# Activation blocks of seven experts turned by transfers and VectorE in place of TensorE

## The chip, the cores and the metric

One core of one Trainium2 chip runs the whole program. The metric is the device time of one execution in microseconds (us), as a median over several runs.

## The reference

Two layers on 256 rows of width 1024, all in float32. Layer 0 has sliding-window and forgetting attention and a dense SwiGLU; layer 1 has differential attention and then a mixture of eight experts, of which each row uses two. Each sublayer ends in a layer norm. The change touches only the experts:

```python
def swiglu(x, w_gate, w_up, w_down):
    return jnp.dot(jax.nn.silu(jnp.dot(x, w_gate)) * jnp.dot(x, w_up), w_down)
...
    def expert_block(args):
        xb, e = args
        return swiglu(xb, w_gate[e], w_up[e], w_down[e])
```

With D = 1024 and 3584 hidden columns an expert has three weight matrices of 14.7 MB each.

## The kernel before

**Units.** Weights stream from HBM in units of 128 x 2048 float32, 1 MB each. The sync engine (SP) loads them into 14 slots of `raw`, one after the other in one queue, each as soon as VectorE has finished with what was in the slot (line 416). ScalarE rounds a unit to float32r (`whi`, helper `hi`, line 1107), VectorE subtracts to get the remainder (`wlo`, helper `lo`, line 1434), and TensorE multiplies with three products per tile (`three`, lines 564 to 566). `whi` and `wlo` have three places, so unit j+3 can be rounded only when TensorE has finished unit j.

**An expert.** `EXP_ORDER` lists its 42 units: for each of seven blocks `c` of 512 hidden columns two units "gate" and two "up", and two "down" units that multiply the finished block. Before, the down units of block c-1 follow the gate and up units of block c. Experts 0 to 6 run in a loop on each engine (`expert(e)`), expert 7 is written out (`last`); a second pass (`again`) exists for the case that an expert gets over 128 rows and isn't executed here.

**A block.** Its 128 rows (partitions) x 512 columns lie in two PSUM banks. After the second up unit ScalarE writes silu of the gate sum to `htmp` and VectorE multiplies by the up sum (`gated`; semaphores `m_silu`, `m_h`; lines 1351 and 1834). TensorE then turns the block, four 128 x 128 tiles, into PSUM bank 4 (`hidden_t`, line 1013; semaphore `m_tr`), after the second gate unit of the next block. ScalarE rounds it into `hth` (`hidden_hi`, line 1355, `m_hi`), VectorE takes the remainder into `htl` (`hidden_lo`, line 1839, `m_lo`), and the down units wait for `m_lo`.

**Order.** Every engine's program is written out: at place j of the list ScalarE and VectorE handle unit j+3 and then whatever else stands at j. GpSimd (POOL), a queue of its own, fetches the next expert's rows from DRAM (`xg` from `x_slots`, four transfers, line 535), and VectorE turns them in 32 x 32 squares (`rows_turned`, line 1808) at places `ROWS_TURN`. Rows get into `x_slots` by four indirect transfers (line 527), and POOL waits for their landing (`x_put`) before the first fetch. SP also writes each expert's output rows (`y_rows`, line 445).

Of the kernel before, what the change touches and what calls it, by code (L numbers as in the profile page):

```python
# [30 lines left out]
P = 128  # L31
D = 1024
TOK = 256
# [91 lines left out]
TAIL_BANKS = (7, 4, 0, 2)  # L125
ROWS_TURN = (PER_EXP - 10, PER_EXP - 9)
PICK_AT = (26, 29, 32, 35)
# [3 lines left out]
def trunk(nc, x_in, w_dense, w_moe, cst, bias_cst, vec_rows, sinks, b_forget, lam_rows, subln, w_router, out):  # L131
    with ExitStack() as ctx:
# [3 lines left out]
        def sem(name):  # L136
            return ctx.enter_context(nc.semaphore(name))
# [85 lines left out]
        def expert_hidden(c, f):  # L223
            if c < EC - 1:
                return hth[:, f * P:(f + 1) * P], htl[:, f * P:(f + 1) * P]
            return xth[:, f, P:TOK], xtl[:, f, P:TOK]

        def expert_hidden_all(c):
            if c < EC - 1:
                return [t[:, :].rearrange("p (k n) -> p k n", k=4) for t in (hth, htl)]  # L230
            return [t[:, 0:4, P:TOK] for t in (xth, xtl)]

# [94 lines left out]
        m_hi = sem("expert_hidden_hi")  # L327
        m_lo = sem("expert_hidden_lo")
        xr_out = sem("x_rows_written")
        y_out = sem("expert_out_rows_written")  # L330
# [83 lines left out]
        def _(sp):  # L414
# [67 lines left out]
        def _(pool):  # L482
# [77 lines left out]
        def _(pe):  # L560
# [446 lines left out]
            def expert(e, last=False, again=False):  # L1007
# [14 lines left out]
                for j, (what, c, half) in enumerate(EXP_ORDER):  # L1022
# [76 lines left out]
        def _(act):  # L1099
# [248 lines left out]

            def gated(e, j, c):
                act.wait_ge(w_used, e * PER_EXP + (N_DENSE + j + 1))  # L1350
                A(htmp[:, :], ps[c % 2][:, :], ACT.Silu).then_inc(m_silu, 1)

            def hidden_hi(e, c):
                act.wait_ge(m_tr, e * EC + (c + 1))
                A(expert_hidden_all(c)[0], ps[4][:, :].rearrange("p (k n) -> p k n", k=4), ACT.Copy).then_inc(m_hi, 1)

            def expert(e, last=False, again=False):
                for j, (what, c, half) in enumerate(EXP_ORDER):
                    s, n = moe_slot(j + SPLIT_AHEAD)
                    if (what, half, c) == ("up", 1, EC - 1):  # L1360
                        gated(e, j, c)
                    if j == PER_EXP - 4:
                        hidden_hi(e, EC - 1)
# [17 lines left out]
                    if (what, half) == ("up", 1) and c < EC - 1:  # L1381
                        gated(e, j, c)
                    if (what, half) == ("gate", 1) and c:
                        hidden_hi(e, c - 1)
                    if j == PER_EXP - 3 and not last:
                        gathered(e + 1)
# [35 lines left out]
        def _(dve):  # L1422
# [408 lines left out]

            def gated(e, c):
                dve.wait_ge(m_silu, e * EC + (c + 1))
                dve.tensor_tensor(htmp[:, :], htmp[:, :], ps[2 + c % 2][:, :], ALU.mult).then_inc(m_h, 1)

            def hidden_lo(e, c):
                dve.wait_ge(m_hi, e * EC + (c + 1))
                h, l = expert_hidden_all(c)
                dve.tensor_tensor(l, ps[4][:, :].rearrange("p (k n) -> p k n", k=4), h.bitcast(F32),
                                  ALU.subtract).then_inc(m_lo, 1)  # L1840
# [8 lines left out]
            def expert(e, last=False, again=False):  # L1849
                for j, (what, c, half) in enumerate(EXP_ORDER):  # L1850
# [8 lines left out]
                    if (what, half, c) == ("up", 1, EC - 1):  # L1859
                        gated(e, c)  # L1860
                    if j == PER_EXP - 4:
                        hidden_lo(e, EC - 1)
# [4 lines left out]
                    if (what, half) == ("up", 1) and c < EC - 1:  # L1867
                        gated(e, c)
                    if j in ROWS_TURN and not (last or again):
# [9 lines left out]
                    if (what, half) == ("gate", 1) and c:  # L1879
                        hidden_lo(e, c - 1)  # L1880
# [202 lines left out]
```

## Time and profile before

| | |
|---|---|
| median of 3 runs | 1396.49 us (1396.47 to 1397.69) |
| the profiled execution's own time | 1397.27 us |
| span from its first to its last instruction | 1395.5 us |
| mean granted TensorE clock | 0.997 |
| TensorE busy | 1375.8 us, 99% |
| VectorE busy | 1128.7 us, 81% |
| ScalarE busy | 958.4 us, 69% |
| GpSimd busy | 53.3 us, 4% |
| DMA | 444.77 MB, mean 319 GB/s |

The experts run from about 434 us to the end. The profile is one execution. Its engines are PE (matmul), PEld (weight load of TensorE), DVE (VectorE), ACT (ScalarE), POOL (GpSimd) and SP (sync); a q behind the name is the engine's instruction queue, where issues of transfers stand. Of the span, 99% is PE busy, but the ends of matmuls are modelled, so a stretch is better measured from the start of one matmul to the start of another.

### The profile page before, as it was taken

Reading aid. Unit: us, or ns where it says so; the run is one execution under the profiler, and the core shown is the slowest. Engines: PE = TensorE matmul, PEld = TensorE weight load, DVE = VectorE, ACT = ScalarE, POOL = GpSimd, SP = SyncE. Lnnn points to the kernel's source line nnn. Section 1 sums busy time; section 2 is a strip of 40 time slices with the busy share of each in tenths; the row PEclk is TensorE's granted clock in tenths of the full one; section 3 lists DMA queues with packets and bytes.
Section 4 is the critical chain, followed back from the end, with each engine's and each line's share of the span. In section 5 each row is a group of like instructions: output and inputs, shape, how many; then the busy total and the mean of one; then the engine's idle time right before and its main releaser. Section 6 shows DMA issues by size and latency. Waiting matters only on the chain.

```text
span 1395.5 us, 18790 instructions
## 1 busy us (share of the span) xinstructions
PE 1375.8 (99%) x6942; PEld 1156.8 (83%) x6942; DVE 1128.7 (81%) x1007; ACT 958.4 (69%) x892; POOL 53.3 (4%) x74
## 2 busy tenths in 40 slices
PE   9999999999999999999999999999999999999996
PEld 9988888889888888888888888888888888888874
DVE  5647555565668889889988998988998898899997
ACT  6655544455657777777877777777777777778774
POOL 1200000000003000000000000000000000000200
PEclk9999999999999999999999999999999999999998
DMA  9834655535157999999999999999999999999950
GB/s 369 355 120 182 212 181 181 185 147 192 51 212 317 394 421 396 423 421 400 416 417 377 369 391 375 371 417 381 369 380 391 373 372 414 375 368 370 393 239 32
DMA packets 65266, 444.77 MB, mean 319 GB/s; under 512 B 7800, under 2 KB 8080, under 8 KB 13760
## 3 DMA queue, kind: packets, MB, share of 16 engines
q1 hardware_dynamic: 60192, 425.96, 77.9%
q0 software_dynamic: 4880, 18.08, 3.7%
q8 instruction: 32, 0.52, 0.1%
q14 instruction: 18, 0.15, 0.0%
q10 hardware_dynamic: 144, 0.07, 0.0%
HBM read 431.48 MB, written 12.59 MB: 318 GB/s over the span
## 4 chain that ended last, share of the span: by engine, by line
PE 92%; DVE 5%; ACT 2%; issue 0%; DMA 0%; SPq 0%; DVEq 0%; ACTq 0%
PE ps L564 26%; PE ps L566 26%; PE ps L565 26%; PE ps L623 6%; PE ps L624 3%; PE ps L1013 2%; DVE wlo L1434 1%; ACT raw L1163 1%; ACT whi L1107 1%; PE ps L776 1%; PE ps L718 1%; DVE raw L1469 1%; PE ps L593 1%; ACT biasb L1142 0%; DVE x L1601 0%
## 5 line engine op out<-in xcount | busy, mean ns | idle before, releaser
L1434 DVE TENSOR_TENSOR wlo<-raw,whi 128x2048 fp32r<-128x2048 f32 x396 | 904.7, 2290 | 169.6 <-ACT whi L1107 168.9
L1107 ACT ACTIVATE whi<-raw 128x2048 fp32r<-128x2048 f32 x397 | 760.3, 1918 | 234.2 <-PE ps L566 227.9
L564 PE MATMUL ps<-whi,xt 128*128 128x512 f32 (+1 forms) x1096 | 432.4, 395 | 2.8 <-DVE wlo L1434 1.7
L566 PE MATMUL ps<-whi,xt 128*128 128x512 f32 (+1 forms) x1096 | 425.8, 388 | 0.0
L565 PE MATMUL ps<-wlo,xt 128*128 128x512 f32 (+1 forms) x1096 | 425.2, 388 | 0.0
L564 PEld LDWEIGHTS ps<-whi,xt 128*128 128x128 f32 x1096 | 205.9, 188 | 48.8 <-DVE wlo L1434 6.7
L566 PEld LDWEIGHTS ps<-whi,xt 128*128 128x128 f32 x1096 | 205.8, 188 | 43.4
L565 PEld LDWEIGHTS ps<-wlo,xt 128*128 128x128 f32 x1096 | 206.1, 188 | 40.2
L564 PE MATMUL ps<-whi,hth 128*128 128x512 f32 x464 | 181.6, 391 | 0.5 <-DVE wlo L1434 0.5
L566 PE MATMUL ps<-whi,htl 128*128 128x512 f32 x464 | 180.8, 390 | 0.0
L565 PE MATMUL ps<-wlo,hth 128*128 128x512 f32 x464 | 180.6, 389 | 0.0
L623 PE MATMUL ps<-xt,whi 128*128 128x512 f32 x352 | 124.7, 399 | 0.3 <-issue 0.3
L564 PEld LDWEIGHTS ps<-whi,hth 128*128 128x128 f32 x464 | 87.1, 188 | 18.7 <-DVE wlo L1434 0.7
L566 PEld LDWEIGHTS ps<-whi,htl 128*128 128x128 f32 x464 | 87.1, 188 | 18.5
L565 PEld LDWEIGHTS ps<-wlo,hth 128*128 128x128 f32 x464 | 87.2, 188 | 17.6
L624 PE MATMUL ps<-xt,wlo 128*128 128x256 f32 x352 | 98.8, 281 | 0.0
L623 PEld LDWEIGHTS ps<-xt,whi 128*128 128x128 f32 x352 | 66.1, 188 | 16.8 <-ACT xt L1122 0.5
L624 PEld LDWEIGHTS ps<-xt,wlo 128*128 128x128 f32 x352 | 66.5, 189 | 0.3
L564 PE MATMUL ps<-xt,whi 128*128 128x256 f32 x232 | 66.4, 286 | 0.3 <-issue 0.3
L565 PE MATMUL ps<-xt,whi 128*128 128x256 f32 x232 | 65.6, 283 | 0.0
L566 PE MATMUL ps<-xt,wlo 128*128 128x256 f32 x232 | 65.6, 283 | 0.0
L564 PEld LDWEIGHTS ps<-xt,whi 128*128 128x128 f32 x232 | 44.4, 192 | 1.7 <-issue 0.9
(258 smaller groups left out, 847.3 us busy)
## 6 DMA issues: line engine op xcount, KB each, us to landing
raw<-w_moe SPq DMA_DIRECT2D x336, 1024.0 KB, 7.7
raw<-w_dense SPq DMA_DIRECT2D x61, 1024.0 KB, 4.8
x_slots<-hth POOLq DMA_DIRECT2D x16, 256.0 KB, 13.1
raw<-vec_rows POOLq DMA_DIRECT2D x4, 1024.0 KB, 6.8
y_rows<-work SPq DMA_DIRECT2D x8, 512.0 KB, 8.5
biasb<-x_slots POOLq DMA_DIRECT2D x28, 128.0 KB, 6.9
raw<-w_dense SPq DMA_DIRECT2D x4, 512.0 KB, 6.9
x<-x_in SPq DMA_DIRECT2D x2, 512.0 KB, 5.3
```

The source lines that it names most:

```text
L564: mm(o, lh, rh, start=start, stop=False)
L565: mm(o, lh, rl, start=False, stop=False)
L566: return mm(o, ll, rh, start=False, stop=stop)
L593: r = pe.transpose(ps[bank][:, i * P:(i + 1) * P], src[:, tb, kt * P:(kt + 1) * P], ident)
L623: mm(ps[bank + b][:, :], h[:, kt, c], xt[:, kt, :, :], start=kt == 0, stop=False)
L624: r = mm(ps[bank + b][:, 0:TOK], l[:, kt, c], xth[:, kt, :], start=False, stop=kt == KT - 1)
L718: r = mm(bank[:, c0:c0 + nk], q, kk, start=True, stop=True)
L776: r = mm(o, PT[g][:, kt, h * P:(h + 1) * P], v, start=kt == 0, stop=kt == qblk)
L1013: r = pe.transpose(ps[4][:, i * P:(i + 1) * P], htmp[:, i * P:(i + 1) * P], ident)
L1107: A(unit(whi, j), raw[:, slot * UNIT:(slot + 1) * UNIT], ACT.Copy).then_inc(hi_rdy, 1)
L1163: A(PROB[g][:, h, 0:nk], PROB[g][:, h, 0:nk], ACT.Exp, bias=negm[:, g % 2, h:h + 1], accum_out=sm[:, g % 4, h:h + 1]).then_inc(e_rdy, 1)
L1434: dve.tensor_tensor(unit(wlo, j), raw[:, slot * UNIT:(slot + 1) * UNIT], unit(whi, j).bitcast(F32), ALU.subtract).then_inc(lo_rdy, 1)
```

## The change

In experts 0 to 6, blocks 0 to 5 are no longer turned by TensorE. `gated` writes them in another column order to `h_rows` (two buffers), sixteen transfers of 32 partitions x 128 columns (16 KB each) move them to `h_moved`, eight issued by SP (semaphores `h_in`) and eight by POOL (`h_in2`), VectorE turns 32 x 32 squares into `h_turned` (`hidden_squares`), and `hidden_hi` and `hidden_lo` read that in place of PSUM. Block 6 and expert 7 are turned by TensorE as before. The down units of a block come one block later, so the weight stream is in another order too. In the new list the last up unit of blocks 0 to 6 stands at 3, 7, 11, 17, 23, 29 and 35, and the down units of blocks 0 to 6 begin at 12, 18, 24, 30, 36, 38 and 40. VectorE turns at 8, 12, 16, 22, 28 and 34; ScalarE rounds one place later; VectorE takes the remainder at 9, 13, 18, 24, 30 and 36. `ROWS_TURN` moves to 31 and 32, and TensorE turns block 6 after unit 37 in place of 38.

```diff
-    if _c:
-        EXP_ORDER += [("down", _c - 1, 0), ("down", _c - 1, 1)]
-EXP_ORDER += [("down", EC - 1, 0), ("down", EC - 1, 1)]
+    if _c > 1:
+        EXP_ORDER += [("down", _c - 2, 0), ("down", _c - 2, 1)]
+for _c in (EC - 2, EC - 1):
+    EXP_ORDER += [("down", _c, 0), ("down", _c, 1)]
+
+MOVED = EC - 1
+UP_END = [EXP_ORDER.index(("up", _c, 1)) for _c in range(EC)]
+MOVE_AT = {UP_END[_c] + 4: _c for _c in range(MOVED)}
+SQUARES_AT = {UP_END[_c] + 5: _c for _c in range(MOVED)}
+HIDDEN_AT = {UP_END[_c] + 6: _c for _c in range(MOVED)}
+REST_AT = {UP_END[_c] + (6 if _c < 2 else 7): _c for _c in range(MOVED)}
...
-ROWS_TURN = (PER_EXP - 10, PER_EXP - 9)
+ROWS_TURN = (PER_EXP - 11, PER_EXP - 10)
...
+        h_rows = [htmp[:, :], spare[:, 512:1024]]
+        h_moved = [spare[:, 1024:1536], spare[:, 1536:2048]]
+
+        def hidden_move(engine, c, groups, done):
+            for q in groups:
+                for u in range(4):
+                    engine.dma_start(h_moved[c % 2][32 * q:32 * q + 32, P * u:P * u + P],
+                                     h_rows[c % 2][32 * u:32 * u + 32, P * q:P * q + P]).then_inc(done[c % 2], 16)
+
+        h_turned = [acc[:, 0, 0:512], acc[:, 0, 512:1024]]
...
+                    if j in MOVE_AT:
+                        sp.wait_ge(m_h, e * EC + (MOVE_AT[j] + 1))
+                        hidden_move(sp, MOVE_AT[j], (0, 1), h_in)
                     sp.wait_ge(lo_rdy, e * PER_EXP + (N_DENSE + j + 1))
                     load(w_moe[e * PER_EXP + (SLOTS + j)], moe_slot(SLOTS + j)[0])
...
+                for c in range(MOVED):
+                    pool.wait_ge(m_h, (n - 1) * EC + c + 1)
+                    hidden_move(pool, c, (2, 3), h_in2)
...
-                    if (what, half) == ("gate", 1) and c:
+                    if (what, half) == ("gate", 1) and c and (last or again):
                         hidden_t(c - 1)
-                    if j == PER_EXP - 4:
+                    if j == PER_EXP - 5:
                         hidden_t(EC - 1)
...
+            def hidden_squares(e, c):
+
+                dve.wait_ge(h_in[c % 2], e * (128 * MOVED // 2) + 128 * (c // 2 + 1))
+                dve.wait_ge(h_in2[c % 2], e * (128 * MOVED // 2) + 128 * (c // 2 + 1))
+                if c == 0:
+                    dve.wait_ge(x_put, 16 * 2 * TB)
+                if c > 1:
+                    dve.wait_ge(m_lo, e * EC + (c - 1))
+                dve.transpose(h_turned[c % 2].rearrange("p (f u s) -> p f u s", f=4, u=4),
+                              h_moved[c % 2].rearrange("p (u f r) -> p f u r", f=4, u=4)).then_inc(m_tr, 1)
...
                     if j < PER_EXP - 3 or not last:
                         lo(e * PER_EXP + (N_DENSE + j + SPLIT_AHEAD + 1), j, moe_slot(j + SPLIT_AHEAD)[0])
                     if (what, half) == ("up", 1) and c < EC - 1:
-                        gated(e, c)
+                        gated(e, c, not (last or again))
+                    if j in SQUARES_AT and not (last or again):
+                        hidden_squares(e, SQUARES_AT[j])
+                    if j in REST_AT and not (last or again):
+                        hidden_lo(e, REST_AT[j], True)
```

On ScalarE `gated` and `hidden_hi` change in the same way, `hidden_hi` standing behind the rounding of unit j+3 at the places `HIDDEN_AT`.

## Rows read from the trace of the kernel before

**Rows 1.** The page: busy us (share of the span) x instructions of each engine.
```profile
PE 1375.8 (99%) x6942; PEld 1156.8 (83%) x6942; DVE 1128.7 (81%) x1007; ACT 958.4 (69%) x892; POOL 53.3 (4%) x74
```

**Rows 2.** The page: the chain that ended last, shares of the span by line.
```profile
PE ps L564 26%; PE ps L566 26%; PE ps L565 26%; PE ps L623 6%; PE ps L624 3%; PE ps L1013 2%; DVE wlo L1434 1%; ACT raw L1163 1%; ACT whi L1107 1%; PE ps L776 1%; PE ps L718 1%; DVE raw L1469 1%; PE ps L593 1%; ACT biasb L1142 0%; DVE x L1601 0%
```

**Rows 3.** Waits, whole span: waiter and releaser: us in total, times, longest.
```profile
DVE wlo L1434 <- ACT whi L1107: 168.9, 268, 5.8
...
PEld ps L564 <- DVE wlo L1434: 7.5, 14, 1.1
```

**Rows 4.** Timeline of PE in expert 0: start, us, engine, line, operation.
```profile
451.23 0.39 PE L566 MATMUL ps<-whi,xt 128*128 128x512 f32 x1
451.46 0.60 PE L1013 MATMUL ps<-con,htmp 128*128 128x128 f32 x4
451.81 0.47 PE L564 MATMUL ps<-whi,xt 128*128 128x512 f32 x1
```

**Rows 5.** Timeline of ACT in expert 0, units 8, 9, 11 and 14.
```profile
451.65 1.92 ACT L1107 ACTIVATE whi<-raw 128x2048 fp32r<-128x2048 f32 x1 [0.80 <-PE ps L566]
...
454.84 1.92 ACT L1107 ACTIVATE whi<-raw 128x2048 fp32r<-128x2048 f32 x1 [0.78 <-PE ps L566]
...
460.28 1.92 ACT L1107 ACTIVATE whi<-raw 128x2048 fp32r<-128x2048 f32 x1 [0.32 <-PE ps L566]
...
468.44 1.92 ACT L1107 ACTIVATE whi<-raw 128x2048 fp32r<-128x2048 f32 x1 [0.80 <-PE ps L566]
```

**Rows 6.** Timeline of DVE in expert 0: block 0, and units 7 and 11.
```profile
450.38 0.68 DVE L1834 TENSOR_TENSOR htmp<-htmp,ps 128x512 f32<-128x512 f32 x1
450.97 2.28 DVE L1434 TENSOR_TENSOR wlo<-raw,whi 128x2048 fp32r<-128x2048 f32 x1
...
462.31 2.29 DVE L1434 TENSOR_TENSOR wlo<-raw,whi 128x2048 fp32r<-128x2048 f32 x1
```

**Rows 7.** Groups by line, whole span: busy us, mean ns of one.
```profile
L1013 PE MATMUL ps<-con,htmp 128*128 128x128 f32 x224 | 33.5, 271 | 0.0
...
L1808 DVE STREAM_TRANSPOSE ps<-biasb 128x512 f32<-128x512 f32 x14 | 9.9, 708 | 0.0
```

**Rows 8.** Weight loads by SP, line 416: issued in 448 to 454, then 960 to 980.
```profile
DMA to landing us min/median/max: 27.8/28.1/28.4
...
DMA to landing us min/median/max: 4.7/4.8/4.9
```

**Rows 9.** Output rows by SP, line 445: all seven, then the one of 440 to 450.
```profile
L445 SPq DMA_DIRECT2D y_rows<-work x7: 356/356/371, 443.9 to 1150.6; - x7
...
DMA to landing us min/median/max: 23.4/23.4/23.4
```

**Rows 10.** POOL: timeline in expert 0; line 535 landings at 460 to 470, 640 to 1140.
```profile
448.63 2.67 POOL L527 DMA_INDIRECT x_slots<-acc,x_to  x1 [0.30 <-issue]
464.45 2.29 POOL L535 DMA_DIRECT2D biasb<-x_slots  x4 [13.15 <-DMA x_slots<-acc,x_to]
...
DMA to landing us min/median/max: 6.4/8.0/9.8
...
DMA to landing us min/median/max: 4.8/6.6/11.0
```

**Rows 11.** Stretch 600 to 640 (last: DMA share, GB/s); POOL's queue, 760 to 780.
```profile
600.00:640.00 40.00, 40.00 (x184) 33.09 (x183) 35.26 (x19) 29.36 (x20) 0.00 (x0) 1.00 1.01 423
...
q0 software_dynamic: 192, 0.52, 9.5%
```

**Rows 12.** Stretches at the end (columns as before, third from last PEclk); first matmuls (line 571).
```profile
1385.00:1388.00 3.00, 0.00 (x0) 0.00 (x0) 3.00 (x8) 2.11 (x4) 0.00 (x0) 0.80 0.02 5
1388.00:1390.00 2.00, 0.00 (x0) 0.00 (x0) 1.93 (x5) 0.85 (x3) 0.00 (x0) 0.50 0.04 8
...
L571 PE MATMUL ps<-con x80: 272/275/275, 6.0 to 425.5; 128*128 128x128 f32 x80
...
L571 PE MATMUL ps<-htmp x18: 274/421/581, 1.1 to 4.7; 128*128 128x128 f32 x18
```

More of the change, by code:

```diff
@@ L223, in expert_hidden @@
         def expert_hidden(c, f):
-            if c < EC - 1:
+            if c < EC - 1 and c % 2 == 0:
                 return hth[:, f * P:(f + 1) * P], htl[:, f * P:(f + 1) * P]
-            return xth[:, f, P:TOK], xtl[:, f, P:TOK]
+            f0 = 4 if c < EC - 1 else 0
+            return xth[:, f0 + f, P:TOK], xtl[:, f0 + f, P:TOK]
         def expert_hidden_all(c):
-            if c < EC - 1:
+            if c < EC - 1 and c % 2 == 0:
                 return [t[:, :].rearrange("p (k n) -> p k n", k=4) for t in (hth, htl)]
-            return [t[:, 0:4, P:TOK] for t in (xth, xtl)]
+            f0 = 4 if c < EC - 1 else 0
+            return [t[:, f0:f0 + 4, P:TOK] for t in (xth, xtl)]
+        h_rows = [htmp[:, :], spare[:, 512:1024]]
[6 more added lines that the diff above has]
+        h_turned = [acc[:, 0, 0:512], acc[:, 0, 512:1024]]
         def part_bank(q):
@@ L328, in trunk @@
         m_lo = sem("expert_hidden_lo")
+        h_in = [sem(f"expert_hidden_first_half_moved_{i}") for i in range(2)]
+        h_in2 = [sem(f"expert_hidden_second_half_moved_{i}") for i in range(2)]
         xr_out = sem("x_rows_written")
@@ L1347, in gathered, with gated, hidden_hi @@
                 r.then_inc(ga_hi, 1)
-            def gated(e, j, c):
+            def gated(e, j, c, moved):
                 act.wait_ge(w_used, e * PER_EXP + (N_DENSE + j + 1))
-                A(htmp[:, :], ps[c % 2][:, :], ACT.Silu).then_inc(m_silu, 1)
-            def hidden_hi(e, c):
+                if moved:
+                    A(h_rows[c % 2].rearrange("p (q f r) -> p f q r", q=4, f=4),
+                      ps[c % 2][:, :].rearrange("p (f q r) -> p f q r", q=4, f=4), ACT.Silu).then_inc(m_silu, 1)
+                else:
+                    A(htmp[:, :], ps[c % 2][:, :], ACT.Silu).then_inc(m_silu, 1)
+            def hidden_hi(e, c, moved=False):
                 act.wait_ge(m_tr, e * EC + (c + 1))
-                A(expert_hidden_all(c)[0], ps[4][:, :].rearrange("p (k n) -> p k n", k=4), ACT.Copy).then_inc(m_hi, 1)
+                A(expert_hidden_all(c)[0], (h_turned[c % 2] if moved else ps[4][:, :]).rearrange("p (k n) -> p k n", k=4),
+                  ACT.Copy).then_inc(m_hi, 1)
             def expert(e, last=False, again=False):
@@ L1360, in expert @@
                     if (what, half, c) == ("up", 1, EC - 1):
-                        gated(e, j, c)
-                    if j == PER_EXP - 4:
+                        gated(e, j, c, False)
+                    if j == PER_EXP - 5:
                         hidden_hi(e, EC - 1)
@@ L1381, in expert @@
                     if (what, half) == ("up", 1) and c < EC - 1:
-                        gated(e, j, c)
-                    if (what, half) == ("gate", 1) and c:
+                        gated(e, j, c, not (last or again))
+                    if (what, half) == ("gate", 1) and c and (last or again):
                         hidden_hi(e, c - 1)
+                    if j in HIDDEN_AT and not (last or again):
+                        hidden_hi(e, HIDDEN_AT[j], True)
                     if j == PER_EXP - 3 and not last:
@@ L1859, in expert @@
                     if (what, half, c) == ("up", 1, EC - 1):
-                        gated(e, c)
-                    if j == PER_EXP - 4:
+                        gated(e, c, False)
+                    if j == PER_EXP - 5:
                         hidden_lo(e, EC - 1)
@@ L1867, in expert @@
                     if (what, half) == ("up", 1) and c < EC - 1:
-                        gated(e, c)
+                        gated(e, c, not (last or again))
[3 more added lines that the diff above has]
+                        hidden_lo(e, REST_AT[j], True)
                     if j in ROWS_TURN and not (last or again):
@@ L1878, in expert @@
                         dve.tensor_copy(slot_tok[:, :], ps[7][:, 256:257]).then_inc(ix_rdy, 1)
-                    if (what, half) == ("gate", 1) and c:
+                    if (what, half) == ("gate", 1) and c and (last or again):
                         hidden_lo(e, c - 1)
```

13 lines of the change are left out of this document (9 added, 4 removed).

## The prediction

> **What bounds the kernel now.** I read the page first: TensorE is busy for 99% of the span and VectorE for 81% [rows 1], and the chain that ended last runs nearly all over the matmul lines, with 2% on the turning line L1013 [rows 2]. The waits say the same: TensorE waited for VectorE's remainders 14 times, 7.5 us in all, while VectorE waited 168.9 us for ScalarE, which itself waits for TensorE to give a place back [rows 3]. So a microsecond off TensorE's stream is a microsecond off the time, as long as the three engines' loop and the transfers keep up. What a change costs is therefore read where the new waits end: in VectorE's queue (which makes `wlo`) and at `m_lo`.
>
> **Slack of the loop.** Call T(j) the moment at which ScalarE takes unit j+3, just after TensorE ended unit j. A unit lasts 2.72 us: units 11 and 14 are taken at 460.28 and 468.44 [rows 5], a third of 8.16. Rounding takes 1.92 [rows 5], the remainder 2.29 [rows 6], with 0.03 between: it is there at T(j)+4.24. TensorE begins the next unit some 0.19 before the T of the last (its next matmul could start 0.23 after 451.23, ScalarE starts at 451.65 [rows 4, 5]), so it needs unit j+3 at T(j)-0.19+5.44 = T(j)+5.25. VectorE may be 1.0 us late, not more.
>
> **Part 1, the turning removed: -19.7 us.** Without turning T advances by 2.72; over one turning it advances 454.84-451.65 = 3.19 [rows 5]. One block costs 0.47 us. (PE's own starts give 0.58-0.23 = 0.35 and a slower next matmul [rows 4], together 0.44.) Six blocks in seven experts are 42, 42 x 0.47 = 19.7; by the lower figure 18.5. The 224 matmuls of line 1013 at 271 ns [rows 7] would make far more, 42 x 4 x 0.271 = 45.5, but they overlap; the starts decide. The Trainium skill, page "VectorE: DVE Perf Modes", section "Rules for kernel authors", advises TensorE for a 128 x 128 transpose when PSUM will do, which speaks against this change, and its section on the three paths gives TensorE 390 ns (bf16): by that figure the four-tile turnings would cost 168 x 0.39 = 65.5 us, where the trace has 19.7.
>
> **Part 2, VectorE's new work: hidden, 0.** Each block adds one turn of squares, 0.708 [rows 7], of which 0.09 overlaps the neighbour as `gated` does (450.38+0.68 against 450.97 [rows 6]): 0.62. A unit with one extra step takes VectorE 2.20+0.60, 2.8 to 2.85, 0.1 more than TensorE's 2.72. The longest run of such units is places 28 to 32 (squares, `gated`, remainder, two `rows_turned`): 5 x 0.12 = 0.6, under the 1.0 of slack. If the regrouped reads and writes run 20% slower (no row shows them), it costs some tenths an expert. I take 0 here, at most +3 in all. ScalarE's work is the same in amount and is hidden as before. SP issues 8 transfers a block at 0.36 [rows 9], 2.9 us in 16 us in which it only waits; the loads behind them go out 3 us later, with 11 units in hand.
>
> **Part 3, block 5 comes too late for unit 38: +14.2 us.** The down units of block 5 are 38 and 39, directly behind those of block 4, but VectorE takes its remainder at place 36, behind the remainder of unit 39. That one can't be there before T(36)+4.24; ScalarE has silu of block 6 and the rounding of block 5 in the same two units (two of 0.6 beside two of 1.92 in 5.44), which makes it some 0.1 later. Then 0.68 less overlap: `m_lo` comes at T(36)+5.0. TensorE would begin unit 38 at T(36)-0.19+2.72 = T(36)+2.53. The gap is 2.5 us; the turning of block 6 (0.47, after unit 37) falls into it. Net 2.03, times seven experts 14.2. Before, place 38 took the last block's remainder ahead of the unit's own; now that holds for block 6 only. The other blocks have a place or more to spare: block 0 is due at unit 12 and is taken at 9, at T(9)+4.9, where TensorE comes at T(9)+5.25.
>
> **Part 4, the first move stands behind the weight queue: +15.3 us.** At the start of the experts the loads are far behind: those issued at 448 to 454 land 28.1 us later, while in 960 to 980 it is 4.8 [rows 8]. Is that the queue, or only the loads? The write of output rows, of another kind but issued by SP at 443.9, also took 23.4 us [rows 9]: whatever SP issues waits its turn. POOL's transfers of that time land after 6.4 to 9.8 [rows 10], so its queue is not behind that backlog. Now block 0 of expert 0: `m_h` comes at 450.38+0.68 = 451.1 [rows 6]. SP's eight moves go out until 454 and stand behind a load issued at 450.5, which lands at 478.5; the moves at about 479.5. POOL's half comes no earlier: POOL first waits for the rows' landing until 464.45, issues four fetches in 2.29 [rows 10], then eight moves at 0.55 until 471.2; with 6.4 to 9.8 to land, 477.6 to 481. VectorE stands at the squares from the end of unit 11's remainder, 462.31+2.29 = 464.6 [rows 6], less the turning that is gone: 464.1. Queued behind it on VectorE are units 12 and up, which TensorE wants. TensorE ends unit 11 at 468.44-0.47-0.19 = 467.8 [rows 5]. After 479.5 come the squares (0.62), unit 12's remainder (2.20), block 0's remainder (0.68), and unit 12 is a down unit that needs both: 483.1. TensorE is idle for 15.3 us; with the two landings as bounds, 13.5 to 17. In the kernel before nothing in TensorE's path waits for this queue within 30 us, so nothing is paid back later.
>
> **Part 5, the clock after it: +1.8 us.** At the end the granted clock goes from 1.00 to 0.80 and 0.50 (2.4 to 1.2 GHz) once TensorE has stopped [rows 12]. The first 18 matmuls of the kernel, from 1.1 to 4.7 us, lasted 421 ns in the median and up to 581, where the same line later takes 275 [rows 12]: about 3.6 us at half pace, 1.8 lost. I take the same here once; between 0 and 4.
>
> **Part 6, the blocks after: +2 us.** While TensorE stands, the queue shortens, but SP keeps loading up to 12 units ahead, so the moves of blocks 1 to 5 still stand behind 4 to 5 MB. `m_h` comes at T(j)+4.8 and VectorE reaches the squares at T(j+5)+4.24: 13.0 us for issue and landing. After the stop the loads in front of each block's moves land 11 to 12.5 us after `m_h`: a margin under 1.5, plus the 1.0 of slack. Does the queue drain? TensorE needs 117.8 an expert (443.9 to 1150.6 over six [rows 9]), less 6 x 0.47, plus 2.03: 117.0. The transfers: 42 MiB at 423 GB/s, the rate while the queue is full [rows 11], 104.1; output rows 1.2; the fetched rows 1.9 (0.52 MB in 9.5% of 20 us [rows 11]). The moves, 0.26 MB a block, cost 0.62 at that rate, 0.95 at the price of the fetch (32 partitions too, but pieces twice as large, nearest in kind), 1.9 if half the piece doubles that. With 0.95 the sum is 112.9: it drains 4 us an expert, and small waits of experts 0 and 1 make about 2 us; bounds 0 and 6.
>
> **The sum.** -19.7 + 0 + 14.2 + 15.3 + 1.8 + 2.0 = +13.6 against the profiled execution's 1397.3 (span 1395.5 and 1.8 around it): 1410.9. The median lies 0.8 below that execution: 1410.1.
>
> **Rivals.**
> (a) The transfers bind, slower still. At 1.9 us a block the sum of part 6 is 118.6 an expert against 117.0, and the moves' landing holds VectorE in every expert: +1.6 x 7 = 11, 1421. POOL's half can do it alone: eight issues are 4.4 us, and a landing of 11.0, the longest [rows 10], makes 15.4 against 13.0, so 2.4 less 1.0 = 1.4 late; in a third of the 42 blocks that is 20, 1430. For it: 672 small transfers. Against: a landing of 6.6 in the median gives 11.0 us, in time; it decides at 14 us.
> The Trainium skill, page "DMA: Bandwidth & Descriptors", section "Bandwidth", calls transfers under 64 KB descriptor-dominated and gives 0.68 us for 4 KB and 0.95 for 64 KB: an estimate of sixteen at 0.7 one after another would be 11.2 us a block, 67 an expert, 57 over what TensorE's pace leaves, and about 1810 us. No run here shows transfers of 16 KB in a row; if they overlap the rule doesn't bite, and a bit of (a)'s chance is for it.
> (b) Faster: the moves of block 0 are not held by the queue (they land within 13 us, as POOL's fetches did). Then parts 4 to 6 vanish: 1410.1-19.1 = 1391.0. Against: the 23.4 us of the output rows, and POOL's start at 466.7, which alone gives a wait. It decides whether landing is before 465.
> (c) No wait at unit 38, if VectorE runs further ahead than I read: 1410.1-14.2 = 1395.9, no change. Against: unit 39 can't be rounded before unit 36 has ended, whatever VectorE does.
> (d) Neither, the change as it is meant: 1397.3-19.7-0.8 = 1376.8.
>
> **How the numbers follow.** My case 0.60, with 1400 to 1420 for itself (part 4 +-2, part 3 +-3, part 6 and clock +-4); (a) 0.20; (b) 0.08; (c) 0.07; (d) 0.05. Faster by over 0.2% (2.8 us, about what a measurement here can tell): (b) and (d), 0.13. Within it: (c) and a sliver of mine, 0.09. Slower: 0.78. The range leaves out (b) and (d) below and the far part of (a) above: 1394 to 1428.
>
> **What would show it.** L1013 with 56 matmuls in place of 224; 42 squares more on VectorE. Part 4: one idle time of TensorE of 14 to 17 us near 468, VectorE's squares waiting for a transfer, a granted clock of 0.5 in that stretch. Part 3: seven idle times of about 2.5 us on TensorE, one an expert, ended by VectorE's remainder of a block. Parts 2 and 6: no waits for transfers from expert 2 on; many of them would speak for (a). I am wrong if SP's small moves overtake its loads, or if VectorE's regrouped steps take much over 0.7 us.

## The result and the profile after the change

| | before | after |
|---|---|---|
| median of 4 runs | 1397.09 us (1396.47 to 1397.99) | 1472.94 us (1472.10 to 1473.60) |
| span of the profiled execution | 1395.5 us | 1470.7 us |
| mean granted TensorE clock | 0.997 | 0.980 |

The ratio is 1.0542 (95% interval 1.0529 to 1.0555): 75.8 us slower. The forecast was 13.6 us slower, with a range up to 1428, so the side was right and the size far off. First the page of the kernel after: busy us (share) x instructions, the chain that ended last by engine and by line, and the weight loads with their median us to landing.

```profile
PE 1385.9 (94%) x6774; PEld 1144.3 (78%) x6774; DVE 1145.9 (78%) x1049; ACT 956.3 (65%) x892; POOL 218.3 (15%) x410
...
PE 49%; DMA 22%; DVE 12%; SPq 9%; issue 4%; ACT 3%; DVEq 0%; ACTq 0%
PE ps L593 13%; PE ps L595 12%; PE ps L594 12%; DMA biasb<-htmp 12%; DMA biasb<-biasb 9%; SPq L249 8%; DVE wlo L1470 7%; PE ps L652 6%; PE ps L653 3%; ACT whi L1136 2%; DMA raw<-w_dense 1%; ACT raw L1192 1%; PE ps L805 1%; PE ps L747 1%; DVE htmp L1872 1%
...
raw<-w_moe SPq DMA_DIRECT2D x336, 1024.0 KB, 12.7
```

TensorE was busy for 99% [rows 1] and made nearly the whole chain [rows 2]; now it makes half. The moves (`biasb<-htmp` and `biasb<-biasb` are the two buffers) and SP's issuing of them (L249) are 29% of it. The waits of the kernel after, as in [rows 3] (us in total, times, longest):

```profile
DVE acc L1885 <- DMA biasb<-htmp: 49.0, 15, 19.5
...
DVE acc L1885 <- DMA biasb<-biasb: 25.0, 19, 2.2
```

That is 74.0 us in 34 of 42 blocks, where I had foreseen one wait and a few small ones. The lines L1470, L1872, L1885 and L1891 here are the remainder, `gated`, `hidden_squares` and `hidden_lo`. VectorE (DVE) in the third expert, the stretches of its squares, shows what nearly every block looks like:

```profile
746.06 0.68 DVE L1872 TENSOR_TENSOR htmp<-htmp,ps 128x512 f32<-128x512 f32 x1
...
762.71 0.71 DVE L1885 STREAM_TRANSPOSE acc<-biasb 128x512 f32<-128x512 f32 x1 [2.83 <-DMA biasb<-htmp]
...
780.30 0.71 DVE L1885 STREAM_TRANSPOSE acc<-biasb 128x512 f32<-128x512 f32 x1 [1.73 <-DMA biasb<-biasb]
...
798.21 0.71 DVE L1885 STREAM_TRANSPOSE acc<-biasb 128x512 f32<-128x512 f32 x1 [2.06 <-DMA biasb<-htmp]
```

**Where the 75 us of span lie.** The issues of `y_rows` stand one expert apart. Before, they come at 443.9 and then every 117.8 us; after, at 444.9, 591.3, 717.3, 843.5, 969.7, 1094.0 and 1220.1. Expert 0 takes 146.4, the next five 125.8 each. From the last of them to the end it is 250.6, before 244.9. So: 1.0 up to the experts, 28.6 in expert 0, 5 x 8.0 = 40.0 in the next five, 5.7 in the last two: 75.3.

### The profile page after: what moved, and what is told of

Read it like the earlier page. It is cut to its first block, busy times and chain, and to the rows that moved or that the text cites. A ratio compares the mean times of both kernels' runs of the same rounds, so it can differ in the third digit from the quotient of the medians.

```text
span 1470.7 us, 19231 instructions
## 1 busy us (share of the span) xinstructions
PE 1385.9 (94%) x6774; PEld 1144.3 (78%) x6774; DVE 1145.9 (78%) x1049; ACT 956.3 (65%) x892; POOL 218.3 (15%) x410
## 4 chain that ended last, share of the span: by engine, by line
PE 49%; DMA 22%; DVE 12%; SPq 9%; issue 4%; ACT 3%; DVEq 0%; ACTq 0%
PE ps L593 13%; PE ps L595 12%; PE ps L594 12%; DMA biasb<-htmp 12%; DMA biasb<-biasb 9%; SPq L249 8%; DVE wlo L1470 7%; PE ps L652 6%; PE ps L653 3%; ACT whi L1136 2%; DMA raw<-w_dense 1%; ACT raw L1192 1%; PE ps L805 1%; PE ps L747 1%; DVE htmp L1872 1%
## 5 line engine op out<-in xcount | busy, mean ns | idle before, releaser
L1470 DVE TENSOR_TENSOR wlo<-raw,whi 128x2048 fp32r<-128x2048 f32 x396 | 899.3, 2284 | 153.2 <-ACT whi L1136 151.6
L593 PE MATMUL ps<-whi,xt 128*128 128x512 f32 (+1 forms) x1288 | 515.9, 401 | 48.3 <-DVE xt L1891 24.8
L594 PE MATMUL ps<-wlo,xt 128*128 128x512 f32 (+1 forms) x1288 | 505.4, 392 | 0.0
L595 PE MATMUL ps<-whi,xt 128*128 128x512 f32 (+1 forms) x1288 | 505.3, 392 | 0.0
L593 PEld LDWEIGHTS ps<-whi,xt 128*128 128x128 f32 x1288 | 244.9, 190 | 124.6 <-DVE wlo L1470 48.6
L595 PEld LDWEIGHTS ps<-whi,xt 128*128 128x128 f32 x1288 | 244.9, 190 | 52.9
L594 PEld LDWEIGHTS ps<-wlo,xt 128*128 128x128 f32 x1288 | 245.4, 191 | 47.2
L249 POOL DMA_DIRECT2D biasb<-htmp x168 | 82.4, 499 | 381.1 <-DVE htmp L1872 380.4
L593 PE MATMUL ps<-whi,hth 128*128 128x512 f32 x272 | 108.0, 397 | 19.8 <-DVE htl L1891 19.4
L249 POOL DMA_DIRECT2D biasb<-biasb x168 | 82.2, 497 | 254.0 <-DVE biasb L1872 246.4
L595 PE MATMUL ps<-whi,htl 128*128 128x512 f32 x272 | 106.8, 393 | 0.0
L594 PE MATMUL ps<-wlo,hth 128*128 128x512 f32 x272 | 106.7, 392 | 0.0
L1885 DVE STREAM_TRANSPOSE acc<-biasb 128x512 f32<-128x512 f32 x42 | 29.9, 711 | 74.1 <-DMA biasb<-htmp 49.0
L652 PEld LDWEIGHTS ps<-xt,whi 128*128 128x128 f32 x352 | 66.1, 188 | 16.8 <-ACT xt L1151 0.5
## 6 DMA issues: line engine op xcount, KB each, us to landing
raw<-w_moe SPq DMA_DIRECT2D x336, 1024.0 KB, 12.7
```

The costliest lines, as they stand in the source:

```text
L249: engine.dma_start(h_moved[c % 2][32 * q:32 * q + 32, P * u:P * u + P], h_rows[c % 2][32 * u:32 * u + 32, P * q:P * q + P]).then_inc(done[ ...
L593: mm(o, lh, rh, start=start, stop=False)
L594: mm(o, lh, rl, start=False, stop=False)
L595: return mm(o, ll, rh, start=False, stop=stop)
L652: mm(ps[bank + b][:, :], h[:, kt, c], xt[:, kt, :, :], start=kt == 0, stop=False)
L1470: dve.tensor_tensor(unit(wlo, j), raw[:, slot * UNIT:(slot + 1) * UNIT], unit(whi, j).bitcast(F32), ALU.subtract).then_inc(lo_rdy, 1)
```

## The experiments

Two explanations stood against each other for the many waits. "Full": the transfers of an expert take longer in sum than TensorE does, whatever is waited for (the forecast's rival (a), far above its price). "Late": each move only takes too long to land, since it is issued late and stands behind loads. They differ when a move is made but not waited for, and when it gets more time. Times are medians; each ratio is to the kernel before, run beside it (1397.1 to 1397.6 us). Runs e1, e2b, e6 to e9, e11 and e14 move or load something else than the kernel needs, so what they compute is not the reference's.

### The moves taken away: e1 and e6

Without the moves, VectorE turns squares of what `gated` wrote; e6 also takes block 5's remainder ahead of unit 39's.

```diff
-                if j in MOVE_AT: ... hidden_move(sp, MOVE_AT[j], (0, 1), h_in)
-            for c in range(MOVED): ... hidden_move(pool, c, (2, 3), h_in2)
-                dve.wait_ge(h_in[c % 2], ...); dve.wait_ge(h_in2[c % 2], ...)
+                dve.wait_ge(m_h, e * EC + (c + 1))
# e6 also
+                    if REST_AT.get(j) == MOVED - 1 and not (last or again):
+                        hidden_lo(e, MOVED - 1, True)
                     if j < PER_EXP - 3 or not last:
                         lo(...)
```

> The changed kernel without its sixteen transfers a block: VectorE turns the squares straight out of the block as it was written (the output is then not the reference's), at the same places, and nobody waits for a transfer. It gives what the transfers cost in all and what is left. Both theories (late: the transfers' landing comes after VectorE's place; full: the transfers take the 16 DMA engines' time) say the same here: the 19.7 us of TensorE's turnings gone, the wait at unit 38 left at 2.5 us an expert, so 1391 us; if that idle time drops TensorE's clock in every expert as the trace after shows (0.5 for 3.4 us), up to 12 more, 1403.

> e1_no_moves with the remainder of block 5 taken at place 36 ahead of the remainder of unit 39 in place of behind it (the output isn't the reference's, as there). My part 3: the wait at unit 38 (2.2 us here, and half a clock behind it in four experts) goes, so 1398.8 - 7 x 2.0 - 4 x 1.4 = 1379, and the 19.7 us of the turnings show for the first time. Rival: VectorE's fuller queue is what ate the gain; then the time stays within 3 us of 1398.8.

e1: 1398.76 us, ratio 1.0014 (1.0003 to 1.0025). e6: 1376.99, ratio 0.9849 (0.9833 to 0.9866). So all but 1.7 of the 75.8 us come with the moves. e6 is 20.2 under before: that is the turning's worth, 19.7 in the forecast, with VectorE's new work at nothing. The difference of the two, 21.8 us, is block 5 coming late to unit 38. The wait is in the trace of e1 as forecast, 2.2 us in each of seven experts, and behind it stands a cost that I had not put down. Waits of the weight loads (PEld), then two stretches of expert 0 (third number from last: the granted clock):

```profile
PEld ps L587 <- DVE xt L1884: 15.2, 7, 2.2
```

```profile
541.00:545.00 4.00, 3.60 (x11) 2.85 (x12) 3.22 (x3) 0.90 (x1) 0.00 (x0) 0.74 1.00 386
545.00:549.00 4.00, 4.00 (x16) 3.22 (x15) 1.38 (x1) 2.08 (x2) 0.00 (x0) 0.83 1.01 422
```

In four of the seven experts the clock falls to 0.50 (1.2 GHz) for some 3.3 us just after this short stop. TensorE works through that time at half pace: 4 x 3.3 / 2 = 6.6, and 15.2 + 6.6 = 21.8.

### The moves made, but their data not needed: e2b, e7, e8, e9, e11

Here the transfers read a constant and write to buffers that nobody reads; the squares are those of e1. Each is still checked for its landing, but later: before the squares of blocks 3 and 4 VectorE waits for the moves of blocks 0 to 3, and at the end of an expert for the rest. e2b makes all sixteen a block, e7 SP's eight alone, e8 POOL's eight alone. e9 makes four of 128 partitions x 128 columns (64 KB), two by each; e11 two of 32 partitions x 512 columns (64 KB) by SP.

```diff
-    engine.dma_start(h_moved[c % 2][32 * q:32 * q + 32, P * u:P * u + P],
-                     h_rows[c % 2][32 * u:32 * u + 32, P * q:P * q + P])
+    engine.dma_start(h_dump[c % 4][32 * q:32 * q + 32, P * u:P * u + P],
+                     con[32 * u:32 * u + 32, P * q:P * q + P])
# e9, one for each q
+    engine.dma_start(h_dump[c % 4][:, P * q:P * q + P], con[:, P * q:P * q + P])
# e11, one for each q, SP alone
+    engine.dma_start(h_dump[c % 4][32 * q:32 * q + 32, :], con[32 * q:32 * q + 32, 0:512])
# all five, in hidden_squares (shown for e2b)
+                if c in (3, 4):
+                    dve.wait_ge(h_in[c - 3], e * (128 * MOVED // 2) + 256)
+                    dve.wait_ge(h_in2[c - 3], e * (128 * MOVED // 2) + 256)
```

> As e1_no_moves, but the sixteen transfers a block are issued by SP and POOL at their places, with a constant table as their source and dumps that nobody reads; VectorE only makes sure far later that they have landed (the output isn't the reference's). Late: only the waiting hurt, so the time is that of e1_no_moves within 5 us. Full: the transfers fill the DMA engines, the weight loads fall behind, ScalarE comes to wait for weights, and the time stays near 1450.

> e2b_unawaited with SP's eight transfers a block alone, POOL's left out (output not the reference's). Its price a block is read from how fast the queue of weight loads drains: landing of loads (28 us at the start), where 10.3 us an expert go in the kernel before. If price goes with bytes (0.62 us a block for all sixteen), nothing is seen: 1399. If the two halves share the 3.2 us a block that the full queue implies, 1.6 each, the sum is 107 + 10 = 117 an expert, just TensorE's pace: 1399 to 1405 with the landing staying near 25. If SP's half is the dear one (the trace after shows the rate falling to 300 GB/s for five microseconds when it passes), 2.5 us: 122 an expert, about 1425.

> e2b_unawaited with POOL's eight transfers a block alone, SP's left out (output not the reference's). Even shares: as e7. If SP's half is the dear one, POOL's costs 0.7 us a block, the queue drains by 6 us an expert, and the time is that of e1_no_moves, 1399.

> e2b_unawaited with the same 0.26 MB a block in the same 512-byte rows, but as four transfers of 128 partitions x 128 columns, two by SP and two by POOL, in place of sixteen of 32 partitions (output not the reference's). If the price is per byte or per row, it stays that of e2b_unawaited, 1458. If it is per transfer or by the 32 partitions that each touches, it falls to a quarter, 0.8 us a block: 1399 to 1402, and the queue drains.

> e7_sp_half_unawaited with SP's eight transfers of 32 partitions x 128 columns a block replaced by two of 32 partitions x 512 columns: the same 0.13 MB, the same 32 partitions each, a quarter of the count (output not the reference's). If each transfer from SP has its price, the 2.25 us a block fall to 0.6 and the time is that of e1_no_moves, 1399. If the price lies in touching 32 partitions at a time, it stays at 1425.

| | us | ratio (interval) | us per expert |
|---|---|---|---|
| e2b, all sixteen | 1457.72 | 1.0433 (1.0402 to 1.0463) | 127.5 |
| e7, SP's eight | 1425.44 | 1.0199 (1.0178 to 1.0219) | 122.9 |
| e8, POOL's eight | 1398.37 | 1.0008 (0.9998 to 1.0018) | 118.2 |
| e9, four of 64 KB | 1398.97 | 1.0012 (1.0001 to 1.0022) | 118.0 |
| e11, two tall ones by SP | 1400.98 | 1.0029 (1.0018 to 1.0039) | 118.3 |

e2b is still 59 us slower than e1, where "late" had it near e1. But the time alone doesn't settle the question, since the late check was not late enough. VectorE's waits for moves in e2b, then in e7, and ScalarE's for weights in e2b:

```profile
DVE acc L1888 <- DMA acc<-con: 43.7, 11, 6.7
```

```profile
DVE acc L1884 <- DMA acc<-con: 26.1, 11, 5.7
```

```profile
ACT whi L1137 <- DMA raw<-w_moe: 24.2, 20, 2.3
```

In every expert of both runs the squares of block 3 stood for moves of the block before (and at times those of block 4), and those waits are as large as most of what the two runs lose against e1 (59 and 27 us). e8, e9 and e11 have none. What speaks for "full" is the queue. If the moves were only late, the backlog of loads would drain as it does in e1, and faster, since the experts last longer; in e2b it never does, and ScalarE comes to wait for weights 20 times, which neither e1 nor the kernel before shows in the experts. Landing of SP's loads in e2b at 960 to 980 us, where the kernel before had 4.8 in the median [rows 8]:

```profile
DMA to landing us min/median/max: 20.6/27.7/29.5
```

The kernel after says the same of itself. Landing of all its loads issued from 560 to 1290 us:

```profile
DMA to landing us min/median/max: 6.3/12.8/16.6
```

Where the queue has run empty a load lands after 4.7 [rows 8]; here none does in six experts, so it is never empty. e14, below, closes the question.

**The price of a move.** A load's landing time is the backlog in front of it. While that is well above 4.7 us, it shrinks in each expert by TensorE's period less the time that the transfers need. Loads of e1 issued at 460 to 480 us, then at 700 to 720:

```profile
DMA to landing us min/median/max: 25.2/25.9/26.9
...
DMA to landing us min/median/max: 7.6/8.4/9.2
```

17.5 us in 240 us, which are 2.03 periods of 118.2: 8.6 an expert, so without moves the transfers need 109.6. (I had 107.2 from the rate of the full queue.) The same for e8, at 460 to 480 and 1060 to 1080:

```profile
DMA to landing us min/median/max: 29.0/29.2/29.5
...
DMA to landing us min/median/max: 9.1/9.5/10.4
```

19.7 in 5.08 periods is 3.9: they need 114.3, and six blocks make 4.7, 0.8 a block for POOL's eight. e9 gives 25.4 at 520 to 540 and 11.0 at 1060 to 1080, 3.1 an expert, 0.9 a block. e11 gives 28.0 and 22.7, 1.0 an expert, 1.3 a block. In e7 and e2b the backlog doesn't shrink, so the period is what the transfers need, whoever waits: (122.9 - 109.6) / 6 = 2.2 a block for SP's eight, (127.5 - 109.6) / 6 = 3.0 for all; and 2.2 + 0.8 = 3.0. By the same rule the kernel after gives a little less, (125.8 - 109.6) / 6 = 2.7; its moves read and write other buffers than those of e2b, and whether that makes the difference isn't shown. The prices are good to about 0.1 us a block, since the landing time also moves by 1 or 2 us within an expert. A transfer of 16 KB by SP thus takes 0.28 us from all the others, one by POOL 0.10, where its bytes at 423 GB/s [rows 11] are 0.04. Of SP's tall ones (32 partitions, 64 KB) each takes 0.65, so the median of e11, which lies between its two expectations, tells little, and the drain tells that neither the count alone nor the bytes alone set the price.

The packets show one difference between the two queues. Queues on the pages of e8, then of e7: packets, MB, share of 16 engines (q1 is SP's, q0 POOL's; without moves they have 60192 and 4880):

```profile
q1 hardware_dynamic: 60192, 425.96, 77.7%
q0 software_dynamic: 15632, 23.60, 5.1%
```

```profile
q1 hardware_dynamic: 76320, 431.48, 80.0%
q0 software_dynamic: 4880, 18.08, 3.5%
```

336 moves are 16128 packets by SP, 48 each, and 10752 by POOL, 32 each. A price of 2.8 times is more than the packets' 1.5 times; what the rest is stays open.

### More time for the moves, or a shorter queue: e3, e4, e5, e14

e3 takes squares, rounding and remainder of blocks 1 to 4 two places later. e4 turns expert 0 by TensorE. e5 is e6's reordering with the moves left in. e14 loads three quarters of the unit in 294 of the 336 loads of expert weights (all but the first 14 and the last 28).

```diff
# e3
+LATER = (0, 2, 2, 2, 2, 0)
+SQUARES_AT = {UP_END[_c] + 5 + LATER[_c]: _c for _c in range(MOVED)}   # HIDDEN_AT, REST_AT alike
# e4, on each engine
+            for e in range(1):
+                expert(e, plain=True)
+            with dve.Fori(1, N_EXP - 1) as e:
# e14
+                sp.dma_start(raw[:, s * UNIT:s * UNIT + 3 * UNIT // 4], src[:, 0:3 * UNIT // 4]).then_inc(loaded[s], 16)
```

> The changed kernel with squares, rounding and remainder of blocks 1 to 4 two places (5.4 us) later, where their down units leave room. Late: the waits of 1.7 to 2 us before the squares of these blocks go, some 6 us an expert, 42 in all, 1432. Full: the landing moves out with the place, since the loads in front go out sooner; no change, 1465 to 1473.

> The changed kernel with expert 0 written out and its blocks turned by TensorE; experts 1 to 6 as in the change. Expert 0 took about 146 us where it took 118. Late: 28 us less, 1445, if the queue has drained below VectorE's 13 us by expert 1. Full: the queue still holds 17 us of loads at expert 1, the first block there waits some 5 to 7 us, 1452.

> The changed kernel with the remainder of block 5 ahead of unit 39's, the edit that gave 21.8 us where no transfers ran. Full: TensorE's wait at unit 38 was time in which the weight queue caught up, so most of the gain is given back at the squares of the next blocks: 1465 to 1473, a gain under 8. Late (each wait stands for itself): 1473 - 21.8 = 1451.

> The changed kernel, transfers and waits untouched, with every weight load of experts 0 to 6 cut to three quarters of its unit (the rest of the slot keeps old data; the output isn't the reference's). Full: an expert's transfers fall from 126 to about 100 us, under TensorE's 117, the queue empties, the waits at the squares go from expert 1 on, and the time comes down to that without moves plus the first block's wait, 1399 + 17 + 2 = 1418, less where the smaller loads have shortened the first queue too. Late (issue of 5 us and a landing that comes with any transfer, against 13.0): 1455 or more.

**e3**: 1495.14 us, ratio 1.0701 (1.0644 to 1.0757), 22 us above the kernel after. The waits of blocks 1 to 4 went, as "late" had it, but block 5 paid for them all: five microseconds more for four of six blocks brought nothing. That it got worse neither explanation had foreseen. VectorE's waits:

```profile
DVE acc L1886 <- DMA biasb<-biasb: 63.0, 7, 10.4
DVE acc L1886 <- DMA biasb<-htmp: 18.8, 1, 18.8
```

The time that was owed in four or five pieces, some 8 us an expert, is paid in one piece of 9 at block 5, whose squares were not moved. The sum is about the same, 81.8 against 74.0. But TensorE now stands for longer at a time, and the clock stays at half longer behind it: the end of the stop in the third expert and 8 us behind it:

```profile
820.00:824.00 4.00, 0.00 (x0) 0.00 (x0) 0.00 (x0) 0.00 (x0) 0.00 (x0) 0.74 1.01 291
824.00:828.00 4.00, 1.12 (x4) 0.72 (x4) 3.33 (x3) 2.58 (x3) 0.00 (x0) 0.50 1.01 420
828.00:832.00 4.00, 0.99 (x2) 0.83 (x3) 4.00 (x5) 2.13 (x2) 0.00 (x0) 0.50 1.00 418
```

Its mean granted clock is 0.960, against 0.980. During the long stop SP has nothing to load, and the queue even runs empty for a while (in every expert some loads land in 4.7 or 4.8 us), so the 129.0 us an expert of e3 aren't set by the sum of the transfers alone.

**e4**: 1456.78, ratio 1.0426 (1.0370 to 1.0482). That is nearer to the 1452 of "full" than to the 1445 of "late", and slower than both. The first wait isn't gone but comes one expert later, at 11.3 us in place of 19.5, in an expert of 137.0; the next four take 125.5 each, like those of the kernel after. **e5**: 1470.81, ratio 1.0526 (1.0505 to 1.0547). The edit that was worth 21.8 us without the moves is worth 2.1 with them: TensorE gets to the next block sooner and waits there. The squares of block 0, which the kernel after has in time from expert 1 on, now wait 3.1 to 3.4 us in each of these experts. That is how a bound by the transfers looks.

**e14**: 1415.33, ratio 1.0131 (1.0110 to 1.0151). Of all waits of the squares one is left, in expert 0:

```profile
DVE acc L1888 <- DMA biasb<-htmp: 14.0, 1, 14.0
```

With the sixteen moves as they are and a quarter less to load, experts 1 to 5 take 118.2 each, as in e1. It is therefore their sum with the loads that makes the waits of all later blocks, not the moves' own landing.

### POOL alone: e12, e10, e13, and the order alone: e15

```diff
# e12
-                        hidden_move(sp, MOVE_AT[j], (0, 1), h_in)
-                    hidden_move(pool, c, (2, 3), h_in2)
+                    hidden_move(pool, c, range(4), h_in2)
# e10 also (blocks 0, 5 and 6 by TensorE)
-MOVED = EC - 1
+MOVED = (1, 2, 3, 4)
+SQUARES_AT = {UP_END[_c] + 7: _c for _c in MOVED}
# e13 also (expert 0 by TensorE)
-                for c in MOVED:
+                for c in (MOVED if n > 1 else ()):
# e15
+MOVED = ()
```

> The changed kernel with all sixteen transfers of a block issued by POOL. If SP's eight are what fills the queue, the price a block falls from 3.0 to about 1.6 us and what is left is: 1398.8 without moves, one long wait at the first block of expert 0 (POOL is free at 467.8, issues until 476, landing by 484: some 18 us and 2 of clock), and issue and landing of 8 + 5.7 us against 13.0, a wait of up to 1 us a block less slack: 1420 to 1440. If the number of transfers is what counts, whoever issues them: 1465 or more.

> A version meant to beat both: only blocks 1 to 4 are moved (TensorE turns 0, 5 and 6), POOL issues all sixteen transfers of a block and SP none, and the squares stand two places later (18.4 us after the block is written, where POOL needs 8 to issue and 6 to 8 to land). 28 turnings less at 0.47 are 13.2 us; no wait at unit 38; the first block of expert 0 is some 3 us late at the squares: 1387. If sixteen of POOL's transfers are as dear as SP's eight (over 2.2 us a block), the queue of loads stays full: 1400 or more.

> e10_four_by_pool with expert 0 written out and turned by TensorE throughout. There one stall of TensorE in expert 0, ended by POOL's first moves, and the half clock behind it cost some 9 to 10 us; expert 0 gives up four turnings, 1.9 us. So 1391.2 - 9.5 + 1.9 = 1383.6. If the queue of loads, which stayed at 21 us there, is the bound that ate the difference (sixteen small transfers by POOL fill what TensorE's pace leaves), the time stays at 1390 or more.

> The new order of the weight stream and of the down units alone: no block is moved, TensorE turns all seven in every expert. The order costs nothing: 1397 within 2. If it costs (down units of blocks 5 and 6 back to back), up to 7 us more.

**e12**: 1494.74 us, ratio 1.0697 (1.0676 to 1.0719). The first expectation missed. The second had "1465 or more" if the number of transfers fills the queue; the time fits, but the cause is another. If POOL's price is 1.6 a block for sixteen, the transfers need 109.6 + 9.6 = 119.2, and indeed the loads land after 7.2 us in the median: this kernel isn't full. It is late. POOL and VectorE in the third expert:

```profile
728.51 0.68 DVE L1868 TENSOR_TENSOR htmp<-htmp,ps 128x512 f32<-128x512 f32 x1
...
745.47 0.71 DVE L1880 STREAM_TRANSPOSE acc<-biasb 128x512 f32<-128x512 f32 x1 [3.20 <-DMA biasb<-htmp]
```

```profile
729.48 7.84 POOL L249 DMA_DIRECT2D biasb<-htmp x16 [39.70 <-DVE htmp L1868]
```

`m_h` comes at 729.2. Sixteen issues take 7.84 us, up to 8.6 go by until landing, and the squares begin at 745.5, 16.3 us after `m_h`, where 13.0 are to be had. So there are two bounds, and each half of the moves meets one: from SP they are too dear, from POOL they take too long to issue.

**e10** goes between them: four blocks, squares two places later, all by POOL. 1391.20, ratio 0.9956 (0.9940 to 0.9973), 4 us above what was expected. One wait is left, 6.4 us in expert 0, as e13 takes it away: **1384.18 us, ratio 0.9906 (0.9890 to 0.9923)**, no wait of the squares at all, 13 us faster than before and 89 faster than the kernel after. In e13 the loads' landing neither falls nor grows, 21.8 us in the median at 960 to 980, so its period of 116.0 from expert 1 on is again what the transfers need: (116.0 - 109.6) / 4 = 1.6 a block for POOL's sixteen, twice the 0.8 of e8. **e15**, the new order with all blocks turned by TensorE: 1396.58, ratio 0.9996 (0.9986 to 1.0005). The order costs nothing by itself.

## Why the prediction was right or wrong

| step | forecast | measured | from |
|---|---|---|---|
| part 1, turning gone | -19.7 | -20.2 | e6 against before |
| part 2, VectorE's new work | 0 | in the -20.2 | e6 |
| part 3, unit 38 | +14.2 | +21.8 | e1 against e6 |
| parts 4 and 5, first wait, clock | +17.1 | about +21 | see below |
| part 6, blocks after | +2.0 | about +53 | the rest |
| sum | +13.6 | +75.8 | |

The last line but one is a remainder, and the terms don't add as the table has them: once the transfers bind, TensorE's wait at unit 38 is time that they use too. e5 takes that wait away from the kernel after and gains 2.1 us of the 21.8.

**Part 1** held: what counts is the start of the next matmul, not the 271 ns of each turning. By the 390 ns of the Trainium skill's page "VectorE: DVE Perf Modes", section "The three transpose paths", the forecast's estimate was 65.5 us; e6 gives a third of it. The advice of the same page of the Trainium skill to use TensorE (section "Rules for kernel authors") is right for the change as it was made, 75.8 us slower. But VectorE's squares are hidden in e6; it is the moves that are dear, and with four blocks and POOL alone e13 beats the kernel that turns all by TensorE.

**Part 2** held. Regrouped reads and writes are no slower: lines of the kernel after, busy us, mean ns, against 0.68 and 0.708 in [rows 6, 7]:

```profile
L1885 DVE STREAM_TRANSPOSE acc<-biasb 128x512 f32<-128x512 f32 x42 | 29.9, 711 | 74.1 <-DMA biasb<-htmp 49.0 <-DMA biasb<-biasb 25.0
L1891 DVE TENSOR_TENSOR htl<-acc,hth 128x512 fp32r<-128x512 f32 x21 | 14.4, 684 | 0.0
L1872 DVE TENSOR_TENSOR htmp<-htmp,ps 128x512 f32<-128x512 f32 x21 | 14.3, 679 | 0.0
```

But one clause of it was wrong: SP's issues. [Rows 9] gave 0.36 us for a large write; a move takes 0.59, and where the queue is backed up up to 6.3 (line 249 of the kernel after, min/median/max ns):

```profile
L249 SPq DMA_DIRECT2D biasb<-biasb x168: 512/590/6266, 467.5 to 1308.1; - x168
```

**Part 3**: the mechanism and the wait held (2.2 us in e1 against 2.5 less the turning of 0.47). The term was short by what the clock does after a stop of two microseconds, 6.6 us. In the kernel after, where VectorE comes late from its squares besides, the same wait is 3.3 to 3.8 us long.

**Part 4**: the mechanism held, the moves of block 0 do stand behind the weight queue. SP, VectorE and TensorE in expert 0 of the kernel after:

```profile
452.15 9.22 SPq L249 DMA_DIRECT2D biasb<-htmp  x8
```

```profile
484.71 0.71 DVE L1885 STREAM_TRANSPOSE acc<-biasb 128x512 f32<-128x512 f32 x1 [19.54 <-DMA biasb<-htmp]
```

```profile
488.33 0.79 PE L593 MATMUL ps<-whi,hth 128*128 128x512 f32 x1 [19.36 <-DVE htl L1891]
```

19.4 us in place of 15.3. The failed clause is again the issue: eight took 9.22 us and not 2.9, the last going out at about 461, so that the squares began at 484.7 and not at 479.5. **Part 5** held: the clock is at half from 472 until about 492.6, TensorE works only from 488.3 on, and 4.3 us at half pace cost 2.1. Together with part 4: expert 0 takes 146.4, later ones 125.8, 20.6 more.

**Part 6** is the step that failed, and by the table it carries 51 of the 62 us that were missed. It priced a block's moves at 0.95 us, by the fetches of POOL, which the text called "nearest in kind", with 1.9 for the far bound. The runs show 3.0 (e2b). The sum of transfers that I put at 112.9 against TensorE's 117.0 is 109.6 + 6 x 3.0 = 127.6 by e2b, and 125.8 by the kernel after: 10.5 to 12.3 us of the error from the moves, 2.4 from the rest. Eight of the sixteen moves go out by the queue that [rows 10] said nothing about, and they are the dear half, 2.2. POOL's half wasn't priced well either: by its fetches 0.48 for eight, measured 0.8, and 1.6 for sixteen (e13), though that lies under the far bound of 1.9. "It drains 4 us an expert" fell with it, and so the small waits come in every expert, not in two. The queue of loads stays shorter than in e2b (12.7 us against 23.8) because the waits of the squares hold the engines, and with them the loads, back.

**The rivals.** (a), that the transfers bind, is what happened, and I gave it 0.20. It was right in place and low in price: at 118.6 an expert the excess over 117.0 is 1.6, at the measured 125.8 it is 8.8. Its other half, POOL's eight too late, wasn't there (3.9 us of issue and 5.9 of landing), but sixteen by POOL in e12 met it. The estimate from the Trainium skill that stood beside it ("DMA: Bandwidth & Descriptors", section "Bandwidth": transfers under 64 KB are descriptor-dominated) gave about 1810 us; in kind it pointed the right way, since a 16 KB move costs 2.5 to 7 times its bytes, while 0.7 us one after another is far too dear. The same page of the Trainium skill, section "Why small descriptors are slow (HBM only)", says that transfers between SBUF and SBUF don't suffer from small pieces. These small transfers are dear, but the runs don't put it down to their pieces of 512 bytes: e9 has the same pieces and bytes in four transfers of 128 partitions, for 0.9 us in place of 3.0. (b) and (c) fell with the waits in the trace. (d), the change as it was meant, 1376.8, is e6 with 1377.0, but only with the moves left out and block 5's remainder taken earlier.

The chance for "slower" (0.78) stands. The range failed since the unknown price was bounded by rows of another queue: nothing in the trace of before showed a small transfer by SP, and I let a resemblance (32 partitions) set the middle and twice that set the end.

## What to carry to other kernels

A queue of loads that is nearly full has one number that matters: how much of its time is over in each period (here 8.6 us of 118), and a change that adds transfers is priced against that before any latency is looked at. If no row shows a transfer of that size on that queue, put the moves in with nobody needing their data and read how fast the loads' landing time falls; it costs one run and tells about a tenth of a microsecond a block where the median shows nothing. Then look in the trace whether really nobody waits: in e2b and e7 a check meant to be late held VectorE in every expert. When a cost is only handed on (e3, e5), more slack at one place turns up as a longer wait at the next.

## What the runs showed of the hardware

- A transfer of 16 KB, 32 partitions x 512 bytes, within the core's memory takes 0.28 us from the other transfers if SP issues it (e7; 0.24 by the kernel after) and 0.10 if POOL does (e8, e13); these are 48 and 32 packets, and its bytes alone would be 0.04. One of 32 partitions x 2 KB by SP takes 0.65 (e11); four of 128 partitions x 512 bytes, two by each engine, 0.9 together (e9). So SP's two of 64 KB cost at most 0.9 over 128 partitions and 1.3 over 32, although the pieces of the latter are four times as long: the piece of 512 bytes isn't what is dear. How much is the 32 partitions and how much the count isn't settled.
- SP's issue of such a move takes 0.59 us, against 0.33 for a load of 1 MB and 0.36 for output rows, and up to 6.3 when much is queued.
- The granted clock falls to 0.50 after stops of TensorE of only 2.2 us, in four experts of seven (e1), and stays there for about 3.3 us; after the stop of 19.4 us it is at 0.50 until 4.3 us after TensorE has begun again. A stop of 2.2 us thus costs up to 3.9.
